# Delta rule in chunks: the keys' product with the state in the right-hand side of one solve, and the outputs turned behind the last gate block

## The reference

```python
def gdn_chunked(q, k, v, g, beta):
    # in chunks; gc is the running sum of the log decay g within a chunk
    a_in = einsum("id,jd->ij", k * beta, k) * decay
    lmat = where(strict, a_in, 0) + eye
    rhs = concatenate([v * beta, k * beta * exp(gc)])
    u, w = triangular_solve(lmat, rhs)            # two solutions
    def step(state, xs):
        v_new = u - w @ state
        o = q_dec @ state + qk @ v_new
        state = state * g_last + k_dec.T @ v_new
```

## Time and profile before

| what | value |
|---|---|
| time, median of 3 runs | 1641.02 us (1640.03 to 1642.58) |
| span of the profiled execution | 1638.3 us |
| time of the profiled execution itself | not given apart; the median lies 2.7 us above its span |
| PE busy | 1599.2 us, 98% of the span |
| DVE busy | 938.6 us, 57% |
| ACT busy | 675.8 us, 41% |
| POOL busy | 163.7 us, 10% |
| the stretch of the change | about 360 to 455 us |

### The profile page before, as it was taken

How to read it: one execution, slowest core, us unless ns; L and a number is a source line. 1 busy time by engine, 2 the same in 40 slices (tenths; PEclk the granted TensorE clock), 3 DMA queues, 4 the chain that set the end, 5 groups by cost and what they waited for, 6 DMA issues and landing times.

```text
span 1638.3 us, 21431 instructions
## 1 busy us (share of the span) xinstructions
PE 1599.2 (98%) x8303; PEld 1316.2 (80%) x8303; DVE 938.6 (57%) x1397; ACT 675.8 (41%) x1167; POOL 163.7 (10%) x186
## 2 busy tenths in 40 slices
PE   7999999999999999999999999999999999999998
PEld 6877878778888777878888788877787888888886
DVE  5678758856735677766534538565556533333334
ACT  5464456453324433343433445444444422232321
POOL 2012215310001000000000124311000000000000
PEclk9999999999999999999999999999999999999999
DMA  7344223221052986633324132222124233332222
GB/s 195 91 119 127 65 84 97 78 55 51 27 218 90 310 242 231 244 116 90 124 90 141 29 93 76 73 72 65 54 89 129 64 90 102 90 102 92 101 94 72
DMA packets 195401, 179.10 MB, mean 109 GB/s; under 512 B 5982, under 2 KB 175021, under 8 KB 192244
## 3 DMA queue, kind: packets, MB, share of 16 engines
q1 hardware_dynamic: 191888, 169.56, 33.8%
q10 hardware_dynamic: 2276, 6.95, 1.2%
q0 software_dynamic: 1152, 1.44, 0.5%
HBM read 173.58 MB, written 4.58 MB: 109 GB/s over the span
## 4 chain that ended last, share of the span: by engine, by line
PE 72%; DVE 1%; ACT 1%; issue 1%; POOL 0%; DVEq 0%; ACTq 0%
PE acc L656 12%; PE acc L657 12%; PE acc L658 12%; PE acc L697 7%; PE acc L698 7%; PE acc L699 7%; PE acc L1215 2%; PE acc L1217 2%; PE acc L712 2%; PE acc L710 2%; PE acc L711 2%; PE acc L1216 2%; PE acc L1359 1%; PE acc L1343 1%; PE acc L750 1%
## 5 line engine op out<-in xcount | busy, mean ns | idle before, releaser
L2121 DVE TENSOR_TENSOR w_low<-w_raw,w_high 128x1024 fp32r<-128x1024 f32 x230 | 283.7, 1235 | 543.1 <-ACT w_high L1438 542.7
L1438 ACT ACTIVATE w_high<-w_raw 128x1024 fp32r<-128x1024 f32 x224 | 237.3, 1059 | 657.4 <-PE acc L658 405.9
L656 PE MATMUL acc<-h_high,w_high 128*128 128x512 f32 (+1 forms) x1248 | 488.4, 391 | 7.9 <-DVE w_low L2121 2.3
L658 PE MATMUL acc<-h_high,w_low 128*128 128x512 f32 (+1 forms) x1248 | 480.0, 385 | 0.0
L657 PE MATMUL acc<-h_low,w_high 128*128 128x512 f32 (+1 forms) x1248 | 479.7, 384 | 0.0
L656 PEld LDWEIGHTS acc<-h_high,w_high 128*128 128x128 f32 x1248 | 235.2, 188 | 68.9 <-issue 16.7
L658 PEld LDWEIGHTS acc<-h_high,w_low 128*128 128x128 f32 x1248 | 235.0, 188 | 46.9
L657 PEld LDWEIGHTS acc<-h_low,w_high 128*128 128x128 f32 x1248 | 235.4, 189 | 45.9 <-issue 1.7
L697 PE MATMUL acc<-w_high,act_high 128*128 128x512 f32 x496 | 193.7, 390 | 3.6 <-DVE arena L2847 1.5
L699 PE MATMUL acc<-w_high,act_low 128*128 128x512 f32 x496 | 193.0, 389 | 0.0
L698 PE MATMUL acc<-w_low,act_high 128*128 128x512 f32 x496 | 193.0, 389 | 0.0
(11 more groups left out here) (394 smaller groups left out, 1977.8 us busy)
## 6 DMA issues: line engine op xcount, KB each, us to landing
w_raw<-w_in SPq DMA_DIRECT2D x68, 512.0 KB, 3.9
w_raw<-w_mlp SPq DMA_DIRECT2D x64, 512.0 KB, 4.0
w_raw<-w_up SPq DMA_DIRECT2D x44, 512.0 KB, 4.0
arena<-w_ada SPq DMA_DIRECT2D x13, 1024.0 KB, 8.2
w_raw<-w_out SPq DMA_DIRECT2D x24, 512.0 KB, 3.3
early<-w_ada SPq DMA_DIRECT2D x11, 1024.0 KB, 6.2
w_raw<-w_down SPq DMA_DIRECT2D x22, 512.0 KB, 3.3
w_raw<-w_branch_gate SPq DMA_DIRECT2D x16, 512.0 KB, 4.1
```

The costliest lines, as they stand in the source:

```text
L656: pe.matmul(out_, wh, xh, start=start, stop=False)
L658: return pe.matmul(out_, wl, xh, start=False, stop=stop)
L1438: f(WH[:, off % 2, :], RAW[:, off % 4, :], ACT.Copy).then_inc(sem("w_high"), 1)
L2121: tt(WL[:, off % 2, :], RAW[:, off % 4, :], WH[:, off % 2, :].bitcast(F32), ALU.subtract).then_inc(sem("w_low"), 1)
```

## The change

There are no longer two solves. For c of 1 or more PE multiplies the keys as they are with the state (`k_state`), DVE subtracts the scaled values from exp(gc) times that product, in place (`less_state`), and one `solve` gives the new values but for sign and beta, which `solved` applies with the new vector `nbrk` = -brk. The product for w, its copy by ACT (`minus_w`) and `renewed` are gone. The turned keys are now only wanted for the state, scaled at once by DVE `late_k`, so the last chunk does not turn its keys. Chunk 0, whose state is zero, has one solve of the values alone.

The order on the engines changes too. PE does `turn_kv`, `k_state`, `q_state` and `solve` of both halves back to back, then half a gate block, `outputs`, and the other half of the gate block. Gate block 15 stands whole behind the last chunk. All four `o_turn` follow it, and turn into banks (2c + 2) % 8 + q, which lie free then. Row block 0 of w_out follows, tile by tile in the order 1, 2, 3, 0, each behind its banks' outputs, and row blocks 1 and on are whole. On ACT and DVE the split for a gate block moves behind the chunk's updates. `o_gated` for all chunks stands behind the last `o_normed`. SP waits for `d_ks` where it waited for `d_ws`, at the same count, before two loads of w_ada.

```diff
+            def k_state(c, q):
+
+                tc = slice(c * P, (c + 1) * P)
+                pe.wait_ge(sem("d_state"), 2 * c - 1 + q)
                 for h in range(4 * q, 4 * q + 4):
-                    m = pe.matmul(PS[:, b + 2, (h % 4) * P:(h % 4 + 1) * P], KB[:, h, :], GN[:, 8 * c + h, :],
+                    m = pe.matmul(PS[:, 4 + 3 * q, (h % 4) * P:(h % 4 + 1) * P], FT[:, K0 + h, tc], SD[:, h, :],
                                   start=True, stop=True)
-                m.then_inc(sem("d_w"), 1)
+                m.then_inc(sem("d_ks"), 1)
...
+            def solve(c, q):
+
+                if c:
+                    pe.wait_ge(sem("d_rhs"), 2 * c - 1 + q)
+                else:
+                    pe.wait_ge(sem("d_vs"), q + 1)
+                for h in range(4 * q, 4 * q + 4):
+                    m = pe.matmul(PS[:, 4 + 3 * q, (h % 4) * P:(h % 4 + 1) * P], GN[:, 8 * c + h, :], VS[:, h, :],
                                   start=True, stop=True)
                 m.then_inc(sem("d_u"), 1)
...
             for c in range(1, NT):
                 for q in range(2):
                     turn_kv(c, q)
-                gated(11 + c)
+                for q in range(2):
+                    k_state(c, q)
+                for q in range(2):
+                    q_state(c, q)
                 for q in range(2):
                     solve(c, q)
-                if c == NT - 1:
-                    gated(15)
-                for q in range(2):
-                    from_state(c, q)
-                if c == NT - 1:
-                    pe.wait_ge(sem("z_silu"), 16)
-                    o_turn(0)
+                gated(11 + c, [0])
                 for q in range(2):
                     outputs(c, q)
+                gated(11 + c, [1])
+            gated(15)
+            for c in range(NT):
+                o_turn(c)
+            row_block(0, WO_N, 0, WO_A, True, lambda t: pe.wait_ge(sem("d_gated"), 2 * ((t + 3) % 4) + 2),
+                      tiles=[1, 2, 3, 0], used_by=0)
...
+            def less_state(c, q):
+                dve.wait_ge(sem("d_vs"), 2 * c + q + 1)
+                dve.wait_ge(sem("d_ks"), 2 * c - 1 + q)
+                for h in four(q):
+                    m = stt(VS[:, h, :], PS[:, 4 + 3 * q, (h % 4) * P:(h % 4 + 1) * P], ecum[:, c, h:h + 1],
+                            VS[:, h, :], ALU.mult, ALU.subtract)
+                m.then_inc(sem("d_rhs"), 1)
```

## The result

| | before | changed |
|---|---|---|
| median of six runs each, us | 1640.53 | 1629.39 |
| ratio, with its 95% interval | | 0.9943 [0.9932, 0.9954] |
| profiled execution: time, span | span 1638.3 | 1629.13, span 1627.3 |
| mean granted clock of the profiled execution | 0.997 | 0.999 |
| PE busy, rows | 1599.2, 8303 | 1587.8, 8231 |

The change makes the kernel 0.57% faster, by 7.5 to 11.2 us with the interval; the quotient of the two medians, 0.9932, lies at the interval's lower end. The two spans differ by 11.0 us, the forecast gain was 8.5.

What follows compares the result with a forecast made beforehand. PE, busy for 98% of the span, bounds the kernel: 8.0 us of removed work plus 6.0 of old waits less 5.5 of new cost gives 8.5 us, so span 1638.3 becomes 1629.8 and the time 1632.5 us, range 1629.3 to 1637.3.

Steps and rivals of the forecast that it cites:

- PE's list sets the time, and the removed work is 8.0 us: PE in the delta rule's chunks: 7.14 us for the w product and 0.87 for the last chunk's key turning go.
- The waits of before, 6.0 us, go and new ones of 5.3 come: PE's waits in chunks 1 to 3 go; new ones are 1.76 in chunk 2, 1.44 in chunk 3, 2.13 at the end.
- a second half of 1.08 behind a group of 0.89: At the solves of chunks 2 and 3: the second half's right-hand side adds 0.15 us to PE's wait.
- The right-hand side takes 1.12: DVE's `less_state`, which had no row in the trace: 1.12 us, from the state's update of four pieces.
- Rival B: Chunk heads cost more, right-hand side 1.7 us: gain 4.7 us or less, 1635 to 1637.7 us; chance 0.11.
- Part of chunk 3's wait shows at q_state: PE may stop some tenths at `q_state` for ACT's scaled values, and less at the solve.
- Nothing waits before `outputs`: In every chunk DVE needs 2.8 us and more after the last right-hand side; PE has 0.89 + 2.74 of work.
- Rival C: Shorter waits, right-hand side 0.69 us: gain 10.1 us, or 14.0 without any new wait; taken as 1629 us; chance 0.07.
- Rival D: No change, 1641 us: gain given back later, or removed products on PE were hidden behind others; chance 0.06.
- Rival E: Slower: the clock halves behind PE's new waits, one chunk of about 16 us at that level, 1648.5 us; chance 0.06.
- the 1630 to 1635 that had the chance of 0.70: The whole kernel's time: the band around the forecast of 1632.5 us, given chance 0.70.
- the 2.7 us that the forecast adds to the span: Whole kernel: the median of the runs lies 2.7 us above the profiled span, so span 1629.8 becomes 1632.5 us.

Runs made afterwards that it cites:

- e8_out2: Changed kernel with the four products in `outputs` made twice in each chunk, same result; median 1638.77 us, ratio 0.9998 to the kernel before.
- e4_both: Changed kernel with DVE's right-hand side first in each chunk and the split for row block 1 behind the eight `o_gated`; 1625.69 us, ratio 0.9913.
- e6_orderonly: The kernel before's algebra with two solves, put in the order of the change; median 1649.87 us, ratio 1.0065 to the kernel before.

## Why the prediction was right, and where it was not

- **PE's list sets the time, and the removed work is 8.0 us.** Right. 64 rows and the 8 turned ones of the last chunk's keys went, and e8_out2 prices a group at 0.894 us where 0.892 was used.
- **The waits of before, 6.0 us, go and new ones of 5.3 come.** Right to some tenths: the stretch gave 8.47 us, forecast 8.5. Removing all but `q_state`'s part of the new waits gave 4.98, and with that part, 0.34, it is 5.32 for 5.33. One step of the sum was loose: a second half of 1.08 behind a group of 0.89 adds 0.19, where 0.15 was used, twice.
- **The right-hand side takes 1.12.** Right, 2.15 for two. Rival B, which needed 1.7, falls.
- **Part of chunk 3's wait shows at q_state.** Right, 0.34, released by ACT.
- **Nothing waits before `outputs`.** Right. It was called the tightest cover and held.
- **Rival C (no new wait)** did not happen, but the order of e4_both makes it so: it is the kernel that C described, at 1625.7 us for a forecast between 1627 and 1629.
- **Rival D (no change)** falls with e8_out2; the marks from 509 to 1252 us show that nothing is given back later either. The load share that the Trainium skill would have one read (Perfetto Trace Analysis, section Identifying the Most-Contended Engine) was 87% here before and 85% after, 76.54 of 90 us; the time followed PE's list all the same.
- **Rival E (the clock)** was priced as a loss of one whole chunk and given 0.06, on the strength of one wait of 1.55 us at clock 1.00. The trace of before held two rows that speak for it and were not read: waits of 1.96 and 2.25 us, each followed by a clock of 0.91 over 20 us. This is the part of the working that the runs correct. The mechanism is real and small at the new waits: 1.63 us in three of four profiles, never a whole chunk. The sum, which had no term for it, holds for an execution without the fall; with it the changed kernel's gain in the stretch is 6.8 us. The prediction named a clock under 1.00 between 395 and 440 us as a sign of being wrong. The first profile did not show it and the next three did.
- **The median of 1629.39 is 3.1 us under the forecast**, and outside the 1630 to 1635 that had the chance of 0.70: by its number it would be rival C (shorter waits), and the waits were not shorter. 2.5 us of the 3.1 are the profile: the sum was made against one in which the clock fell at two other places, and the one after had none. The 11.0 us between the spans are 8.5 from the change and 2.5 from the clock. The rest is the 2.7 us that the forecast adds to the span. In every listed execution the time lies 1.8 above its own span; the other 0.9 was the distance of one execution from the median of three, and here that distance is 0.3. That the median stayed inside the range, by 0.09 us, is luck: 1631.77 is the median of the 13 executions of this kernel on record.
- **The clock accounts for the spread as well.** The two groups of runs of the changed kernel have means of 1630.4 and 1633.8 us, 3.4 apart, and means of the listed clock of 0.9977 and 0.9956; 0.0021 of 1632 us is 3.4. When each of the 13 executions is reduced by its missing share of the clock, 7.9 us of spread become 1.9 (1625.6 to 1627.5). In the same way the 25 executions of the kernel before that have a listed clock (mean 1639.3 at 0.9971) and these 13 (1632.1 at 0.9966) are 7.2 us apart as measured and 8.0 at an equal clock. These are estimates, since the clocks are listed to 0.001, which is 1.6 us; they agree with the 8.5 of the stretch.

What stays open: why the clock falls behind a given wait in one execution and not in the next, and so whether the two ratios of the changed kernel (0.9943, 0.9964) differ by more than chance in this.

## What to carry to other kernels

Split the interval between two marks on the bounding engine into work and waiting, and do the same for the new order with distances between starts from the trace: here that gave every variant's stretch within 0.3 us as long as the clock held. When work is taken off the bounding engine, look at what stands in front of the new critical instruction on its own engine; two reorderings of DVE's list, with no work removed, were worth 5.0 us beside the 8.5 of the change. Before reading a difference of a few microseconds as the change's, compare marks ahead of it and behind it, and the granted clock between them; over many executions, compare times at an equal clock.

## What was not expected of the hardware

- Waits of the same length on PE are followed by the lower clock in some executions only. Behind 3.31 us, in three profiles of e6_orderonly's kernel, six of nine were followed by groups at 1.26 to 1.71 us in place of 0.89; behind the three short waits at the end of the changed kernel (0.74 and 0.76 us by the trace and one shorter) three of four executions had 0.83 over 10 us, 1.63 us of time. The Trainium skill has that gaps in TensorE's work bring the half clock (TensorE: Matmul & The Clock Gate, section HAM oscillation — how this bites in real kernels). The prediction held this against its trace; the section's own example has longer waits than that, so the 1.55 us at clock 1.00 did not contradict it. The runs agree that gaps can bring the fall, here also waits as short as these, and show that it is not each time: the same gaps in the same kernel passed at 1.00 once.
- The falls came back at a few places of the program: 10 to 20 us, 120 to 140, 335 to 350 and 1260 to 1290, each in some profiles; two of these places stand behind waits of about 2 us (1.96 and 2.25 in the trace of before). Executions of the changed kernel ran from 1628.4 to 1636.4 us; the clocks listed for them go from 0.999 to 0.994 in about the same order.
